# Attention with the values as the stationary operand, low-rank projections moved next to the input projection, and modulation weights read by rows

## The reference

```python
sc, scc = silu(c), silu(c_ctx)
mod_l = split(sc @ ada_w[l] + ada_b[l], 6)            # 1024 x 6144 weights per block
mod_c = split(scc @ ada_w[l] + ada_b[l], 6)
h = rmsnorm(x) * (1 + scale) + shift
aq, ak, av, cq, ckv, kr = split(h @ w_in, (512, 128, 128, 256, 128, 32))
q  = rmsnorm(cq, q_norm) @ w_uq                       # 256 x 768
kv = rmsnorm(ckv, kv_norm) @ w_ukv                    # 128 x 1024
# windowed attention with a sink: 8 heads of 64, 2 key/value heads, 512 keys (latent) or 256 (context)
p = softmax(concat([s_loc, s_ctx, sink]))[..., :-1];  o_a = p @ v
# low-rank ("mla") attention: 8 heads of 96 = 64 + 32 rotated, values of 64
o_b = softmax(q @ k.T * 96 ** -0.5) @ v
x = x + gate * (concat([o_a, o_b]) @ w_out)
```

## Time and profile before

| | us |
|---|---|
| median of 3 runs | 2384.57 (2379.85 to 2390.52) |
| the profiled execution | 2378.21 |
| its span in the trace | 2376.9 |
| TensorE busy | 2170.0 (91%) |
| VectorE, ScalarE, GpSimd busy | 655.4, 352.3, 120.9 |
| mean granted clock of TensorE | 0.965 of full |

### The profile page before, as it was taken

One profiled execution on the slowest core, in us unless ns is written; L12 is line 12 of the kernel. 1 busy time (PEld: TensorE's weight loads), 2 busy tenths in 40 slices (PEclk: granted clock), 3 DMA queues, 4 the chain that ended last, 5 costly groups with the idle time before them and its releaser, 6 DMA issues. The chain is left out here.

```text
span 2376.9 us, 27614 instructions
## 1 busy us (share of the span) xinstructions
PE 2170.0 (91%) x11494; PEld 1338.5 (56%) x11494; DVE 655.4 (28%) x1482; ACT 352.3 (15%) x822; POOL 120.9 (5%) x163
## 2 busy tenths in 40 slices
PE   6987898999999986999989999997599999989998
PEld 2554664656666543444555554554376458858863
DVE  2143332422222213314431211111355231134201
ACT  2052432200000001113420000000121022011000
POOL 4000000010000001000000000000110000000000
PEclk9997999999999998999999999999799999999999
DMA  9364173799999997621199999999644433443441
GB/s 335 127 221 153 46 274 141 279 420 420 420 420 420 421 420 299 215 71 53 54 365 418 419 420 420 420 419 416 224 143 132 125 123 116 144 148 125 142 159 36
DMA packets 154276, 601.48 MB, mean 253 GB/s; under 512 B 15257, under 2 KB 19041, under 8 KB 103456
## 3 DMA queue, kind: packets, MB, share of 16 engines
q1 hardware_dynamic: 144512, 582.98, 63.5%
q0 software_dynamic: 8112, 11.31, 1.4%
q10 hardware_dynamic: 1520, 5.32, 0.6%
HBM read 589.58 MB, written 21.23 MB: 257 GB/s over the span
## 5 line engine op out<-in xcount | busy, mean ns | idle before, releaser
L366 PE MATMUL psum<-ring,h_t 128*128 128x512 f32 (+1 forms) x1024 | 428.3, 579 | 5.1 <-ACT h_t L1076 2.1
L366 PEld LDWEIGHTS psum<-ring,h_t 128*128 128x128 f32 x1024 | 193.8, 193 | 232.2 <-issue 229.0
L399 PE MATMUL psum<-h_t,ring 128*128 128x256 f32 (+1 forms) x1424 | 312.4, 382 | 4.5 <-ACT ff_hid L2576 2.3
L399 PEld LDWEIGHTS psum<-h_t,ring 128*128 128x128 f32 (+1 forms) x1424 | 270.6, 190 | 46.2 <-issue 4.7
L2390 PE MATMUL psum<-ring,h_t 128*64 128x256 f32 x2272 | 260.6, 382 | 1.6 <-issue 1.0
L2390 PEld LDWEIGHTS psum<-ring,h_t 128*64 128x64 f32 x2272 | 157.8, 137 | 87.4 <-issue 10.2
L2390 PE MATMUL psum<-wide,h_t 128*64 128x256 f32 x1664 | 192.8, 385 | 3.7 <-DMA wide<-in_expert_w_dram 2.9
L2390 PEld LDWEIGHTS psum<-wide,h_t 128*64 128x64 f32 x1664 | 115.9, 138 | 68.9 <-issue 10.4
L337 DVE COPY h_t<-psum 128x512 f32<-128x512 f32 (+2 forms) x76 | 50.4, 663 | 315.5 <-PE psum L1944 290.7
L1944 PE MATMUL psum<-gates,h_row_tiles 128*128 128x256 f32 (+1 forms) x512 | 104.8, 359 | 1.4 <-ACT h_row_tiles L337 1.4
L1944 PEld LDWEIGHTS psum<-gates,h_row_tiles 128*128 128x128 f32 x512 | 85.6, 190 | 20.6 <-issue 10.4
(11 more groups left out here) (590 smaller groups left out, 2063.3 us busy)
## 6 DMA issues: line engine op xcount, KB each, us to landing
ring<-in_expert_w_dram SPq DMA_DIRECT2D x210, 1024.0 KB, 24.7
wide<-in_expert_w_dram SPq DMA_DIRECT2D x156, 1024.0 KB, 25.6
ring<-in_ada_w_dram SPq DMA_DIRECT2D x48, 1024.0 KB, 10.9
ring<-in_w_in_dram SPq DMA_DIRECT2D x30, 1024.0 KB, 5.3
ring<-in_diff_w_in_dram SPq DMA_DIRECT2D x12, 1024.0 KB, 15.9
gates<-in_expert_w_dram SPq DMA_DIRECT2D x12, 1024.0 KB, 27.8
x<-in_expert_w_dram SPq DMA_DIRECT2D x12, 1024.0 KB, 28.1
ring<-in_w_gate_dram SPq DMA_DIRECT2D x12, 1024.0 KB, 5.1
```

What stands on the lines that cost most here:

```text
L366: mm = k.nc.tensor.matmul(banks[r][0:m, 0:nn], lhs(k0 + j, r), w[:, j, :], start=(k0 + j == 0), stop=(k0 + j == k_tiles - 1))
L399: mm = k.nc.tensor.matmul(banks[i][0:h, 0:n_rhs], w[:, j, b:b + h], rhs(k0 + j), start=(k0 + j == 0), stop=(k0 + j == k_tiles - 1))
```

## The change

- **Modulation.** `plan_rows` cuts the weights into 8 chunks of 128 rows by 2048 columns (8 KB in a row of DRAM where `plan` had 2 KB). One bank, the eighth, collects all 2048 columns in four blocks of 32 partitions over 8 chunks; one copy, 4 transposes and one bias addition follow.
- **Start.** The two loads of x go to SyncE's queue ahead of the weights; they were on ScalarE's. The transposes of x stand after the chunks 5 and 6.
- **Order of the mixer.** The input projection takes the columns 512 to 1024, 1024 to 1184, 0 to 512. The squares and the root for both low-rank norms run after the second piece. The two low-rank projections, the rotation of their queries and the transposes for the windowed attention follow the third. What stays between swac and mla are the 72 transposes of mla's keys and queries.
- **Attention** in the first block goes through `column_attention`: ScalarE's sums are inverted and VectorE multiplies the probabilities in place, before TensorE turns them. In the mix 64 value columns are stationary and the 128 turned columns move, with two heads side by side in 2 x 64 columns of the array. The result comes out with the head's width on the partitions, straight into `h_t`, so that the 32 transposes of `ab_o` go. The keys of the windowed attention are stored twice, once on either half of the partitions.

```diff
+    def plan_rows(self, w, n_first):
+        for k0 in range(0, D, P):
...
+            self.plan_slot(w[k0:k0 + P, n_first:n_first + 4 * BANK].rearrange("p (j n) -> p j n", n=BANK), (4, BANK),
+                           iter([slot]))
...
-        x_loaded = k.load("act", "x", [(x[:, 0:T_LAT, :], x_dram), (x[:, T_LAT:T_ALL, :], ctx_dram)])
+        x_loaded = k.load("sp", "x", [(x[:, 0:T_LAT, :], x_dram), (x[:, T_LAT:T_ALL, :], ctx_dram)])
...
+            def mix(i):
...
+                for pr in range(pairs):
+                    for j in range(width // P):
+                        for a in range(2):
+                            c = (a * pairs + pr) * width + j * P
+                            mm = nc.tensor.matmul(half(a, pr), units[i]["v"][pr][a][j], probs_t[:, i % 2, c:c + P],
...
+            def sums(i):
+                total = column(i, SUM, 0, heads)
+                dve.wait_ge(*probs_ready.at(2 * (i + 1)))
+                if with_sink:
+                    chain(dve, k.dve_step, v.tensor_tensor(total, total, column(i, SINK, 0, heads), ALU.add))
+                chain(dve, k.dve_step, v.reciprocal(total, total))
+                for h in range(heads):
+                    p = head(probs[:, i % 2, :], h)
+                    ins = v.tensor_scalar(p, p, column(i, SUM, h), None, ALU.mult)
+                    if (h + 1) * width % BANK == 0:
+                        ins.then_inc(sums_ready.sem, 1)
...
+            for i in range(n):
+                if i + 1 < n:
+                    maxima(i + 1)
+                sums(i)
+                if i >= 2:
+                    finish(i - 2)
...
         def product(pe, banks):
-            for k0 in range(0, DK, 4):
+            for kt in range(DK):
                 w = k.take(pe, 4, BANK)
                 for j in range(4):
-                    mm = nc.tensor.matmul(banks[0][32 * j:32 * j + 32, :], silu_c[:, k0 + j, :], w[:, j, :],
-                                          start=(k0 == 0), stop=(k0 + 4 == DK))
+                    mm = nc.tensor.matmul(banks[0][32 * j:32 * j + 32, :], silu_c[:, kt, :], w[:, j, :],
+                                          start=(kt == 0), stop=(kt + 1 == DK))
                 yield mm
                 k.used(k.tensor_done.n)
+                flow.groups(between.get(kt, ()))
...
         for part in parts:
...
+            flow.group(product, [("act", lambda bank: nc.scalar.copy(rows[:], bank))], bank=7)
+            turn(part, now(k.act_evac))
```

More of the change, by code:

```diff
@@ L919, in program @@
         if l == 0:
[L920 removed]
+            for first, cols in AB_ORDER:
+                k.plan(t["ab_w_in"][0], D, cols, first)
+            k.plan(t["mla_w_uq"][0], 256, 768)
+            k.plan(t["mla_w_ukv"][0], 128, 1024)
             ada_part(0, 1)
@@ L1245, in __init__, with group @@
             k.behind(who, stage)
-    def group(self, fill, empties, *_, needs=()):
+    def group(self, fill, empties, *_, needs=(), bank=None):
         k = self.k
-        mine = [(self.at + i) % 8 for i in range(len(empties))]
-        self.at += len(empties)
+        mine = [(self.at + i) % self.turning for i in range(len(empties))] if bank is None else [bank]
+        self.at += len(empties) if bank is None else 0
         for sem, n in needs:
@@ L1329, in turn, with add_bias @@
[L1329 to L1342 removed]
+            def add_bias(bank):
+                first = part * n_blocks
+                return nc.vector.tensor_tensor(
+                    mods[:, l, first:first + n_blocks, :].rearrange("p (j b) q -> p b j q", j=4),
+                    bank.rearrange("p (b j q) -> p b j q", j=4, q=32)[:, :, :, 0:2],
+                    col(f"ada_b{l}", first, n_blocks).rearrange("p (j b) -> p b j", j=4).unsqueeze(3).to_broadcast(
+                        [P, 4, 4, 2]), ALU.add)
@@ L1422, in swa_mla @@
     nc, sb = k.nc, k.sb
+    rows = range(T_ALL)
     with ExitStack() as mix:
-        o = sb("ab_o", [P, T_ALL, D], where=mix)
         mask = sb("swa_mask", [P, T_LAT, 2 * S], where=mix)
@@ new lines, in swa_mla, with turned, fill, empty @@
+        kv = sb("mla_kv", [P, T_ALL, 1024], where=mix)
+        room = gates[:].rearrange("p a s n -> p (a s n)")
+        q = room[:, 0:T_ALL * 768].rearrange("p (t n) -> p t n", t=T_ALL)
+        half = lambda a: slice(64 * a, 64 * a + 64)
+        flow = Flow(k, ("act", "dve"))
+        flow.holder = list(k.holder)
+        turn = turns()
+        def turned(dst, sources, needs, scale=None):
+            who = next(turn)
+            def fill(pe, banks):
+                for i, src in enumerate(sources):
+                    mm = nc.tensor.transpose(banks[0][:, i * P:(i + 1) * P], src, k.ident[:])
+                yield mm
+            def empty(bank):
+                if scale is None:
+                    return copy_by(k, who, dst, bank)
+                if who == "act":
+                    return nc.scalar.activation(dst, bank, ACT.Identity, scale=scale)
+                return nc.vector.tensor_scalar(dst, bank, scale, None, ALU.mult)
+            flow.group(fill, [(who, empty)], needs=needs)
+            return now(k.act_evac if who == "act" else k.dve_evac)
```

397 lines of the change are left out of this document (264 added, 133 removed).

## The result

The changed kernel takes **2321.38 us** (median, 2316.33 to 2326.78) against 2382.21 of the kernel before, measured beside it: ratio **0.9749**, 95% interval 0.9713 to 0.9785. A second measurement of the same two gave 2319.44 against 2380.12, ratio 0.9743 (0.9722 to 0.9763). The profiled execution has a span of 2315.0 us, 61.9 less than the 2376.9 of before.

What follows compares the result with a forecast made beforehand. The mixer was taken as bound by TensorE and waits between its stages. Savings of 4.9 (start), 8.0 (modulations), 26.1 (low-rank), 13.3 (attention) and 4.8 (output) sum to 57 us: 2325 us predicted, range 2307 to 2346.

Steps and rivals of the forecast that it cites:

- What bounds it, and that the shift arrives: Mixer bound by TensorE and by waits between its stages; time saved ahead of the experts comes off the end in full.
- Rival 5: Whole kernel: the experts' transfers set the end whatever the mixer does, 2384 us; chance 0.04.
- Start: Up to the input projection's first matmul: begins at 33.0 us (31.9 to 34.0) instead of 37.91, 4.9 us saved.
- Modulations: Five modulations on the path: each 8.9 us instead of 10.5, 8.0 us saved.
- Low-rank part: Mixer: 42.1 us saved where only 72 transposes stay, 16.0 lost ahead of the windowed attention; net 26.1 (22 to 28).
- Attention: Four attention stages: mix at 1.05 us, 0.8 less; steady steps 3.25 (swa) and 3.9 (mla); 13.3 us saved (3 to 17).
- swa becomes VectorE's: Steady swa unit: VectorE needs 3.25 us, more than TensorE's 3.15, so VectorE sets the step.
- rival 3: Low-rank and mla stages: the denser order keeps the clock at 1.00, mla saves 5 us, 2316 in all; chance 0.15.
- Rival 2: Attention units: each turning waits for VectorE's 1.24 us of sum, inversion and multiplications, 2348 us in all; chance 0.10.
- Rival 4: Attention stages and modulations: TensorE's new waits on VectorE drop the clock to 1.2 GHz, slower, up to 2428 us; chance 0.03.
- The sum: All savings of the mixer's parts together, 57 us, giving 2321 from the profiled execution or 2327.5 from the median.

## Why the prediction was right, and where not

*What bounds it, and that the shift arrives.* Right: 60.4 us at the output projection, 61.9 at the end. Rival 5 is out.

*Start.* The step that was mis-sized: 2.2 us saved instead of 4.9, with the first matmul at 35.75, outside the 32 to 34 named as its sign. The miss of 2.75 us has three parts. The last product ended at 31.39 + 1.06 = 32.45, where 29.7 + 0.9 = 30.6 was forecast: its chunk landed at 30.5, 0.8 late, and the product then stood 0.9 us behind 16 transposes of x, which follow the seventh product without a gap; the sum had put that queue on TensorE at nothing. And the 33.0 taken is 0.8 below what the sum gives with 387 GB/s, 29.7 + 0.9 + 0.6 + 2.6 = 33.8 (the text has 31.9 to 34.0, its own 0.2 not taken off). The turning followed at 33.16 and the rest took 2.59, as forecast. The direction was right for a reason that the term didn't price: with x on the other queue the start is 4.7 us later.

*Modulations.* Right: 8.98 us for 8.9 forecast, 7.7 saved for 8.0.

*Low-rank part.* Right in both its numbers, 42.4 for 42.1 and 16.1 for 16.0, since the steps ahead of the windowed attention were summed from records at full clock, and these ran at 1.00. What the text did not see is that over half of the net gain (15.2 of 26.3, by one profile of each) needs no move.

*Attention.* 17.6 us saved for 13.3, just outside the 3 to 17. The text has no row with 64 stationary and 128 moving columns; the transposes of mla_kv are one, at 0.109. The mix takes 1.02 us, 1.05 forecast, in 0.064 us a record, but that its nearest row gave 0.066 is luck. Those 32 records start in fours at uneven distances, another pattern. Inside the new mix the pace is the lower bound: two heads at once, a pair of records in 0.109 us, 0.055 each; the rest of the 1.02 goes at its two ends, 0.05 us ahead of the second pair and 0.1 where the split changes back. The steady steps are 3.11 and 3.81 (3.25 and 3.9 forecast), the bubble at the end 0.55 as followed. Wrong is "swa becomes VectorE's": TensorE sets the step, VectorE is 0.14 us short of it. The forecast summed VectorE's rows by their durations, which overlap by some 0.08 each. In mla the gain was 10.7 for 6.2. The 4.5 more are mostly the clock, rival 3 in one stage: first scores 3.67 us instead of 5.37 (1.7), scores(2) 1.98 instead of 3.78 (1.8). The first scores took 3.67 with the low-rank part late, too, so their share goes with the breaks inside the old stage and not with its place. The 5.37 stood in the earlier trace rows, was known to be 3.7 at full clock, and was left to a rival with 0.15. mlac gave 0.7 for 1.8: its first scores after the wait ran at a low clock in this execution, and it gave 2.2 in the second (18.4 us).

The Trainium skill, in "TensorEngine Tiling (Array Packing)", Key Properties, has TensorE drained at a change of tiling mode. The trace agrees that it costs something and shows how little: eight transposes ahead of the new mix take 1.03 us from start to start, ahead of the old one 0.92.

*Rival 2* would have needed another order on VectorE: swapped, it costs 32 us. *Rival 4*: the clock didn't fall in steady units; the waits of 0.1 to 0.6 us left it. The argument from swac's 1.00 was weak, for behind the same wait of 3.08 us swac has 0.91 here. The chances have a slip of 0.01 (all but the last two rivals sum to 0.93).

*The sum.* 57 forecast, 61.9 measured in the profiles, 60.8 between the medians: -2.7 at the start, +1.7 in the projection and +1.5 behind the mixer (neither forecast, both by the clock or the spread), +4.5 mla, +0.9 swa, -1.1 mlac.

## What to carry to other kernels

Look for the stretch that is both idle and at a low clock: the breaks in it are paid for twice. Putting its products back to back gave 15 us; moving it away gave 9 more, and 3 in the stage behind it. Work without a place of its own, such as a product that only waits for weights, belongs into the first two units of a pipeline, where the array waits for its first results; there it took some 21 us off. For a step added to an engine near the bound, the order in its queue decides: the same sums and multiplications cost bubbles of 0.2 to 0.6 us a stage behind the next maxima, and 32 us ahead of them. And ask of a small matmul what can run beside it: the mix got shorter because two heads share the array.

## What the runs showed of the hardware

- With 64 stationary and 128 moving columns, for two heads in alternation, two records start 0.007 us apart and the next two 0.109 later. Alone, a transpose of that shape takes 0.109 from start to start, and a record with 128 stationary and 64 moving columns 0.112: which side is the smaller makes little difference here, two at once make a factor of two.
- Rows of VectorE operations of 512 columns overlap: 0.43 us long, 0.35 from start to start.
- The input projection took 63.87 or 65.56 us in different executions of one kernel (granted clock 1.00 and 0.66 between 35 and 40 us), and the eight score records behind swac's wait 1.13 or 2.08. Up to 1.7 us of a stage between two profiles is the clock; mla alone stood at 32.56 us in five of the runs.
- Two transfers of 1 MB for x on ScalarE's queue were there at 16.6 us beside weights in rows of 2 KB on SyncE's, and at 25.0 beside rows of 8 KB. A table of 16 KB on GpSimd's queue was waited for until 27.0 in the second case; in the kernel before its transposes ran at 23.3 without a wait. The shape of the chunks is what differs between the two in what is loaded; no run changes it alone.
- The granted clock of swa, between 0.90 and 0.95 in the runs of the changed kernel, was 1.00 when the wait of 4.08 us at its start was filled. The Trainium skill, in "TensorE: Matmul & The Clock Gate", Part 1, says that an idle array falls to half rate, and here the trace agrees: 2.08 against 1.13 for the scores behind that wait. It does not fall at the same place every time: with the new modulations alone the same four records took 1.13 us behind the same wait, and the stage still had 0.95.
